# Seven of 31 convolution taps on VectorE, with two replica queues and the even layer's end reordered

## The reference

```python
def even_mixer(h, pos, w_in, conv_w, conv_b, ln_w, ln_b, ...):
    a_val, a_gate, q, k, v = _split(h @ w_in, [CONV_CH, CONV_CH, DIFF_QK, DIFF_QK, DIFF_V])
    u = a_val * jax.nn.sigmoid(a_gate)
    u = causal_depthwise_conv(u, conv_w) + conv_b.astype(u.dtype)   # 31 taps, 512 channels
    u = jax.nn.silu(layer_norm(u, ln_w, ln_b))                      # over the 512 channels
    q = partial_rotary(q.reshape(B_, S, 2 * DIFF_HEADS, DIFF_HEAD_DIM), pos)
    k = partial_rotary(k.reshape(B_, S, 2 * DIFF_HEADS, DIFF_HEAD_DIM), pos)
    ...
    o = diff_attention(q, k, v, lam)                 # 4 heads, (softmax 1 - lam * softmax 2) v
    o = rms_norm(o, subln_w) * (1.0 - lambda_init)
    return jnp.concatenate([u, o.reshape(B_, S, DIFF_V)], axis=-1)
...
        x = x + y @ w_out[l]
        h = rms_norm(x, ffn_norm_w[l])
        x = x + (jax.nn.silu(h @ w_gate[l]) * (h @ w_up[l])) @ w_down[l]
```

## Time and profile before

| | before |
|---|---|
| runs, us | 1342.91, 1343.10, 1343.13 |
| median, us | 1343.1 |
| profiled execution, us | 1342.96 |
| its span, first to last instruction, us | 1340.9 |
| PE busy, us | 1319.5 (98%) |
| DVE busy, us | 630.8 (47%) |
| ACT busy, us | 501.0 (37%) |
| mean granted TensorE clock | 0.989 |

### The profile page before, as it was taken

One profiled execution on the slowest core, in us unless ns is written; L12 is line 12 of the kernel. 1 busy time (PEld: TensorE's weight loads), 2 busy tenths in 40 slices (PEclk: granted clock), 3 DMA queues, 4 the chain that ended last, 5 costly groups with the idle time before them and its releaser, 6 DMA issues.

```text
span 1340.9 us, 17222 instructions
## 1 busy us (share of the span) xinstructions
PE 1319.5 (98%) x6507; PEld 1065.5 (79%) x6507; DVE 630.8 (47%) x898; ACT 501.0 (37%) x735; POOL 13.9 (1%) x22
## 2 busy tenths in 40 slices
PE   9999989999999999999999999999999999999997
PEld 6775637888888878888887988888888888878886
DVE  6664623744444442226757337433644444442224
ACT  6344423533333332115464344444433333332111
POOL 0000000000000000000001010000000000000000
PEclk9999988999999999999999999999999999999998
DMA  6222220322222223222321101001322222223221
GB/s 249 85 90 81 68 78 0 126 94 94 94 94 94 94 94 110 94 95 78 102 72 63 48 33 48 32 16 48 125 93 95 94 94 94 94 94 110 94 78 63
DMA packets 34079, 114.08 MB, mean 85 GB/s; under 512 B 4466, under 2 KB 4722, under 8 KB 34034
## 3 DMA queue, kind: packets, MB, share of 16 engines
q1 hardware_dynamic: 34034, 113.44, 25.1%
HBM read 106.90 MB, written 2.10 MB: 81 GB/s over the span
## 4 chain that ended last, share of the span: by engine, by line
PE 93%; ACT 2%; DVE 2%; DMA 1%; SPq 1%; issue 1%; DVEq 0%; ACTq 0%
PE PS L1325 91%; DMA raw<-w_stream 1%; PE PS L1401 1%; SPq L463 1%; PE PS L1740 1%; ACT wring L542 1%; DVE wring L930 1%; DVE hbuf L1173 0%; DVE outT L1319 0%; ACT HH L546 0%; PE PS L1621 0%; DMA reps<-ub 0%; ACT squares L554 0%; ACT G L758 0%; DVE ubuf L901 0%
## 5 line engine op out<-in xcount | busy, mean ns | idle before, releaser
L1325 PE MATMUL PS<-HH,wring 128*128 128x512 f32 x3096 | 730.2, 394 | 0.0
L1325 PEld LDWEIGHTS PS<-HH,wring 128*128 128x128 f32 x3096 | 576.6, 188 | 121.7 <-issue 4.2
L1325 PE MATMUL PS<-AA,wring 128*128 (+1 forms) x1320 | 305.3, 392 | 1.9 <-DVE ubuf L901 1.6
L1325 PEld LDWEIGHTS PS<-AA,wring 128*128 128x128 f32 x1320 | 248.4, 189 | 55.6 <-DVE ubuf L901 2.4
L901 DVE TENSOR_TENSOR ubuf<-PS,rstd 128x512 f32<-128x512 f32 x44 | 30.4, 691 | 198.2 <-PE PS L1325 198.2
L923 DVE TENSOR_TENSOR wring<-raw,wring 128x1024 fp32r<-128x1024 f32 x36 | 44.1, 1226 | 149.6 <-ACT wring L593 149.6
L910 DVE TENSOR_TENSOR wring<-raw,wring 128x1024 fp32r<-128x1024 f32 x88 | 107.5, 1221 | 0.9 <-ACT wring L585 0.4
L930 DVE TENSOR_TENSOR wring<-raw,wring 128x1024 fp32r<-128x1024 f32 x70 | 85.2, 1220 | 42.7 <-ACT wring L542 42.7
L542 ACT ACTIVATE wring<-raw 128x1024 fp32r<-128x1024 f32 x70 | 73.5, 1055 | 76.8 <-PE PS L1325 54.6
L580 ACT ACTIVATE AA<-ubuf 128x512 f32 x44 | 27.9, 633 | 198.2 <-DVE ubuf L908 198.2
L593 ACT ACTIVATE wring<-raw 128x1024 fp32r<-128x1024 f32 x36 | 38.2, 1061 | 155.6 <-PE PS L1325 151.2
(11 more groups left out here) (247 smaller groups left out, 1004.8 us busy)
## 6 DMA issues: line engine op xcount, KB each, us to landing
raw<-w_stream SPq DMA_DIRECT2D x194, 512.0 KB, 3.2
reps<-ub SPq DMA_DIRECT2D x64, 67.5 KB, 2.0
out_t<-outT SPq DMA_DIRECT2D x8, 256.0 KB, 2.2
xT<-x_t SPq DMA_DIRECT2D x3, 512.0 KB, 8.1
first_raw<-w_stream SPq DMA_DIRECT2D x2, 512.0 KB, 9.5
rope<-rope_const SPq DMA_DIRECT2D x1, 576.0 KB, 6.9
consts<-shape_const SPq DMA_DIRECT2D x1, 576.0 KB, 7.7
xT<-x_t SPq DMA_DIRECT2D x2, 256.0 KB, 3.9
```

The source lines that it names most:

```text
L1325: return nc.tensor.matmul(out, lhsT, rhs, start=start, stop=stop)
```

## The change

PE's share of the convolution falls from 31 taps (8 steps) to 24 (6 steps, three parts of two). The other seven taps are multiply-adds of 128 x 512 on DVE, one for each tap and channel block: the first with the bias by TENSOR_SCALAR, six by SCALAR_TENSOR_TENSOR, accumulating in `cacc`, each waiting for the one before. `TAP_SLOTS` says in which slot each stands: one in each slot from 3 to 11, more from 12 on (2, 2, 3, 2, 5, 4 in slots 12 to 17). DVE instead of ACT takes the products out of PSUM and adds them to `cacc`.

DVE sums the four channel blocks (`ln_add`, three adds) so that the layer norm's sum needs one product in place of four, and sums the four squares (`ln_sq_add`) so that the variance needs four small products in place of 16. Of the replicas of c2 and c3, SP issues eight transfers and ACT the other eight. A replica row is 532 floats in place of 540. The end of the layer is written in another order: the layer norm's sum and its centring come ahead of the last head's statistics, the variance ahead of the third output tile's products, and `ln_bc` ahead of the fourth's.

```diff
-GROUPS, SHIFTS, TAP_STEPS = 4, 4, 8
+GROUPS, SHIFTS, TAP_STEPS = 4, 4, 6
+FIRST_DIRECT = SHIFTS * TAP_STEPS
+DIRECT = TAPS - FIRST_DIRECT
+V_DIRECT = V_CONVW + 4 * GROUPS * TAP_STEPS
+TAP_SLOTS = ((3, 4, 5, 6, 7, 8, 8), (9, 10, 11, 12, 13, 14, 14), (12, 13, 14, 15, 15, 16, 16), (16, 16, 16, 17, 17, 17, 17))
...
+        taps = [("tap", (c, k)) for c in range(4) for k in range(DIRECT) if TAP_SLOTS[c][k] == n]
+        for part in range(3):
+            after[part] += taps[part * len(taps) // 3:(part + 1) * len(taps) // 3]
         for part in range(4):
             if kind == "c":
-                order.append(("conv", (slot[1], part)))
+                if part < TAP_STEPS // 2:
+                    order.append(("conv", (slot[1], part)))
...
+        if kind == "c" and slot[1]:
+            order.append(("ln_add", slot[1]))
+        if slot == ("g", 3, 1):
+            order.append(("replicate", 2))
+        if slot == ("c", 1):
+            order.append(("replicate", 3))
...
-                for g in range(GROUPS):
+                for g in range(GROUPS if c < 2 else GROUPS // 2):
                     sp.dma_start(dst[32 * sh:32 * sh + 32, g], ub[c % 2][32 * g:32 * g + 32, sh:sh + REP]).then_inc(sem(f"replicated{c}"), 16)
...
-            elif kind == "conv_evac":
-                act.wait_ge(sem("conv_mm"), a + 1)
-                nc.scalar.activation(cacc[:, a], PS[:, conv_bank(a)], ACT.Identity, bias=vcol(V_CONVB + a)).then_inc(sem("conv_done"), 1)
+            elif kind == "replicate":
+                act.wait_ge(sem("gated"), a + 1)
+                act.wait_ge(tile_used, T_OUT0)
+                for sh in range(SHIFTS):
+                    for g in range(GROUPS // 2, GROUPS):
+                        nc.scalar.dma_start(replicas[a][32 * sh:32 * sh + 32, g], ub[a % 2][32 * g:32 * g + 32, sh:sh + REP]).then_inc(sem(f"replicated{a}"), 16)
...
+            elif kind == "tap":
+                c, k = a
+                src = ub[c % 2][:, FIRST_DIRECT + k:FIRST_DIRECT + k + S]
+                weight = vcol(V_DIRECT + DIRECT * c + k)
+                if k == 0:
+                    dve.wait_ge(sem("gated"), c + 1)
+                    V.tensor_scalar(cacc[:, c], src, weight, vcol(V_CONVB + c), ALU.mult, ALU.add).then_inc(sem(f"direct{c}"), 1)
+                else:
+                    dve.wait_ge(sem(f"direct{c}"), k)
+                    V.scalar_tensor_tensor(cacc[:, c], src, weight, cacc[:, c], ALU.mult, ALU.add).then_inc(sem(f"direct{c}"), 1)
+            elif kind == "conv_evac":
+                dve.wait_ge(sem("conv_mm"), a + 1)
+                dve.wait_ge(sem(f"direct{a}"), DIRECT)
+                V.tensor_tensor(cacc[:, a], cacc[:, a], PS[:, conv_bank(a)], ALU.add).then_inc(sem("conv_done"), 1)
+            elif kind == "ln_add":
...
+                V.tensor_tensor(ln_total[:], cacc[:, 0] if a == 1 else ln_total[:], cacc[:, a], ALU.add).then_inc(sem("ln_added"), 1)
+            elif kind == "ln_sq_add":
...
+                V.tensor_tensor(lnsq[:, 0], lnsq[:, 0], lnsq[:, a], ALU.add).then_inc(sem("ln_sq_added"), 1)
...
             elif kind == "ln_sum":
-                pe.wait_ge(sem("conv_done"), 4)
+                pe.wait_ge(sem("ln_added"), 3)
                 pe.wait_ge(sem("y_scaled"), 2)
-                for c in range(4):
-                    last = mm(PS[:, LN_MEAN], ones, cacc[:, c], c == 0, c == 3)
-                last.then_inc(sem("ln_mean_mm"), 1)
+                mm(PS[:, LN_MEAN], ones, ln_total[:]).then_inc(sem("ln_mean_mm"), 1)
             elif kind == "ln_var_sum":
-                pe.wait_ge(sem("ln_sq"), 4)
+                pe.wait_ge(sem("ln_sq_added"), 3)
                 pe.wait_ge(sem("y_scaled"), 3)
                 for b in range(NB):
-                    for c in range(4):
-                        last = mm(PS[:, LN_VAR, b:b + 1], lnsq[:, c, blk(b)], ones[:, 0:1], c == 0, c == 3)
+                    last = token_sum(PS[:, LN_VAR, b:b + 1], lnsq[:, 0, blk(b)])
```

More of the change, by code:

```diff
@@ L144, in even_order @@
                 order.append(("val_gate", (n, part)))
-            order += after[part]
+            if part < 3 or n < 17:
+                order += after[part]
         order.append({"c": ("conv_evac", slot[1]), "q": ("qk_evac", slot[1]), "g": ("gate_evac", n)}[kind])
-    order += [("sub_lo", 2), ("sub_sum", 1), ("ln_sum", 0), ("sub_ms", 1), ("sub_root", 1), ("sub_rec", 1), ("out_heads", (0, 0, 3)),
-              ("sub_bc", 3)]
-    order += [("ln_centre", c) for c in range(4)]
-    order += [("sub_mul", 3), ("sub_hi", 3), ("sub_lo", 3), ("out_heads", (1, 0, 3)), ("out_heads", (2, 0, 3)), ("ln_var_sum", 0), ("out_heads", (3, 0, 3)), ("ln_var", 0), ("ln_root", 0),
-              ("ln_rec", 0), ("ln_bc", 0), ("out_heads", (0, 3, 4)), ("out_heads", (1, 3, 4)), ("out_heads", (2, 3, 4)), ("out_heads", (3, 3, 4))]
+        if kind == "c" and slot[1]:
[4 more added lines that the diff above has]
+            order.append(("replicate", 3))
+    order += after[3]
+    order += [("sub_lo", 2), ("ln_sum", 0)] + [("ln_centre", c) for c in range(4)]
+    order += [("out_heads", (0, 0, 2)), ("sub_sum", 1), ("out_heads", (0, 2, 3)), ("sub_ms", 1), ("sub_root", 1), ("sub_rec", 1),
+              ("ln_sq_add", 1), ("ln_sq_add", 2), ("out_heads", (1, 0, 3)), ("ln_sq_add", 3), ("sub_bc", 3), ("sub_mul", 3), ("sub_hi", 3),
+              ("sub_lo", 3), ("ln_var_sum", 0), ("out_heads", (2, 0, 3)), ("ln_var", 0), ("ln_root", 0), ("ln_rec", 0), ("ln_bc", 0),
+              ("out_heads", (3, 0, 3))]
+    order += [("out_heads", (n, 3, 4)) for n in range(4)]
     for c in range(4):
@@ L291, in build @@
     ub1, q = at("ub1", [PAD + S + 2], f32, q)
+    ln_total, _ = at("ln_total", [S], f32, q)
     reps, q = at("reps", [GROUPS, REP], f32, q)
@@ L1067, in _ @@
                 diff_combine(a)
+            elif kind == "tap":
[13 more added lines that the diff above has]
+            elif kind == "ln_add":
+                dve.wait_ge(sem("conv_done"), a + 1)
+                if a == 1:
+                    dve.wait_ge(sem("conv_mm"), 2)
+                else:
+                    dve.wait_ge(sem("ln_added"), a - 1)
+                V.tensor_tensor(ln_total[:], cacc[:, 0] if a == 1 else ln_total[:], cacc[:, a], ALU.add).then_inc(sem("ln_added"), 1)
+            elif kind == "ln_sq_add":
+                dve.wait_ge(sem("ln_sq"), a + 1)
+                if a > 1:
+                    dve.wait_ge(sem("ln_sq_added"), a - 1)
+                V.tensor_tensor(lnsq[:, 0], lnsq[:, 0], lnsq[:, a], ALU.add).then_inc(sem("ln_sq_added"), 1)
             elif kind == "ln_centre":
@@ L1476, in _ @@
                                   r == 0, r == TAP_STEPS - 1)
-                if part == 3:
+                if part == TAP_STEPS // 2 - 1:
                     last.then_inc(sem("conv_mm"), 1)
```

10 lines of the change are left out of this document (6 added, 4 removed).

## The result

| | before | after |
|---|---|---|
| runs, us | 1341.71 to 1343.13 (4) | 1328.06, 1328.11, 1330.62, 1331.17 |
| median, us | 1343.0 | 1329.4 |
| profiled execution, us | 1342.96 | 1331.17 |
| its span, us | 1340.9 | 1329.4 |

The ratio is 0.9907, with a 95% interval of 0.9895 to 0.9919. The forecast was 1329.2 us. The profiled execution is the slowest of its four, so its rows show a gain of 11.8 us where the medians show 13.7.

What follows compares the result with a forecast made beforehand. PE, busy 98% of the span, was taken to bound the kernel. Convolution 5.6, replicas 1.2 and end of the layer 8.9, less 1.85 of rotary stalls, gave 13.8 us off 1342.96: 1329.2 us, range 1325 to 1334.

Steps and rivals of the forecast that it cites:

- term for the clock behind the variance: End of the layer: the slow clock over the nine passes behind the variance goes, 1.9 us saved.
- c1 and the replicas: c1's saved part ends in the wait for c2's replicas, which land at 170.4 instead of 171.6: 1.2 us gained.
- Convolution, 5.6: PE drops one part of two tap steps in each of c0, c2 and c3: 3 x 1.86 = 5.6 us saved.
- ACT's eight stand behind the sigmoid: c2's replicas: ACT's transfers start after the last gate's sigmoid at 163.6, the last issued at 168.0, landing at 170.0 at best.
- Rotary products, 1.85: Taps on DVE delay evacuations that rotary products await: 0.77 us in slot 11, 0.92 in 12, 0.15 in 3; 1.85 lost.
- End of the layer, 8.9: Layer norm's end: saves 2.4 us on the sum, 1.2 on the squares' wait, 3.4 on the variance, 1.9 of slow clock.
- DVE's three adds of squares lie beside 12 passes and a spread: Before the variance: PE has other work during DVE's adds, so the wait for squares goes, 1.2 us saved.
- The DMA engines are the limit: Rival: both queues share what one fills, c2's replicas land at 171.6; +1.2 us, 1330.4, chance 0.10.
- The clock stays slow behind the variance: Rival: something in the new order rests PE behind the variance; +1.9 us, 1331.1, chance 0.06.
- the clock is better: Rival: c3's first part, or the stretch behind c2's wait, runs at full clock; 1.7 us less, 1327.5, chance 0.10.
- DVE falls behind: Rival: stalls at the rotary products are twice the forecast and c3's sum comes 2 us late; +3.8, 1333, chance 0.12.
- dear issues: Rival: transfers issued by ACT cost over 1.05 us each and delay PE; at worst 1344 to 1346 us, chance 0.05.

Runs made afterwards that it cites:

- load later: The changed kernel with SP waiting until c2's replicas have landed before issuing tile 24's load and its half of c3: 1323.81 us, ratio 0.9889.
- one queue: The changed kernel with all 16 replica transfers of c2 and of c3 issued by SP, none by ACT: 1327.54 us, ratio 0.9907.
- Taps moved: The changed kernel with taps of c1 and c2 in earlier or later slots, none in slots 11 and 12: 1326.22 us, ratio 0.9904.
- combined: The changed kernel with tile 24 and SP's c3 half held back, no taps in slots 11 and 12, one-column sums spread, variance later: 1322.79 us, again 1321.59.

## Why the prediction was right, step by step

- **The sum was right, in part by parts that offset each other.** Without its term for the clock behind the variance (1.9) it says 11.9 us; work and waits gave 11.8. With the clock's losses taken out of the table of milestones, the stretch to c1 brought 0.5 us for a forecast 0, c1 and the replicas 1.5 for 1.2, c2 and c3 4.1 for 3.7, and the end of the layer 5.9 for 7.0. That the medians show 1.9 us more, just the clock's term, is luck: the profiled pair differs by 0.2 us in clock.
- **Convolution, 5.6: right in work, short in this profile.** c2 and c3 bring 1.0 and 1.1 us in the table of milestones, not 1.86 each. c2's first two parts took 5.34 for 5.04, by the clock; the 24 one-column passes took 3.38 for 2.77, and the slow clock behind them reached past c3's transposes to 188.2. That is 2.0 us more slow clock than in before; without it the two parts bring 4.1.
- **c1 and the replicas, 1.2: right in size, wrong in mechanism.** The step that failed is "ACT's eight stand behind the sigmoid" and are paced by issuing. ACT issues ahead of its arithmetic, so the last one left 2.4 us earlier, at 165.64 for 168.0, and the landing took 4.58 us for 2.0, among other transfers. That the two errors cancel is luck. The gain in this step was 1.5. My doubt, tile 24 and SP's half of c3 beside ACT's half, was the cause of the late landing, and load later priced it at 2.4 us.
  The rule of the Trainium skill (DMA: Bandwidth & Descriptors, Rules for kernel authors) says that more issuing engines bring no bandwidth and save only issue time. Its second half agrees with one queue's 1.5 us. Its first half fits the longer landing at a share of 0.87, but was not tested by itself.
- **ACT's issues: right.** The median was 0.613 us, 0.86 the longest, and c3 did not wait in after.
- **Rotary products, 1.85: 1.41.** 0.81 and 0.60 us for the forecast 0.77 and 0.92; slot 3 cost nothing. Taps moved gave 1.5 to 2.0 back.
- **DVE's taps: right.** Chained ones took 0.747 us for 0.77 (mean of 24). The first took 0.54 for 0.49: the bound from the earlier trace rows was near, not exact. (Slot 8 holds two taps, not one as the section on the change says; c0's are complete there.)
- **End of the layer, 8.9: 9.3, of which 3.4 are the clock's.** Before lost 3.4 us to slow clock in that stretch and after none, where the forecast counted on 1.9. Work and waits brought 5.9 for the forecast 7.0. The step "DVE's three adds of squares lie beside 12 passes and a spread" failed: PE waited 1.01 us, since I checked PE's cover and not the chain from the value product over ACT and DVE. Of the 2.4 for the sum 1.0 to 1.2 are real, of the 3.4 for the variance under 2. The slow clock behind the variance went in one profile of the changed kernel and came in the other, so the term of 1.9 has no ground in the order.
- **The rivals.** "The DMA engines are the limit" was half right: they set the landing, yet two queues still brought time. "The clock stays slow behind the variance" and, for c3's first part, "the clock is better" turned out to vary between executions of one order; the slow stretch behind c2's wait stayed with the wait, as the prediction said. "DVE falls behind" did not come: the stalls were under mine. Nor did dear issues.

## What to carry over

When work is taken off the engine that sets the time, walk the chain of the other engines up to each result it will need, and not only the work it has left to cover it. Before adding a second queue for an urgent transfer, see which transfers that nobody awaits yet go beside it, and hold those back. Where the clock's losses fall differently in each run, compare waits in the trace and the length without those losses; the time alone hides an edit of 1 to 2 us. Count as lost only slow clock in which the engine had work. And look whether one of the slow stretches keeps to a wait: then shortening the wait may pay twice.

## What the runs showed of the hardware

- ACT's sequencer issued transfers while ACT's arithmetic instructions ahead of them were still running: at 161.04 us, beside a copy that ran until 161.79 and ahead of a table load and a sigmoid. The last four came when the sigmoid had ended, and what held them until then is open. An issue took 0.51 to 0.86 us.
- A transfer of 66.5 KB whose median landing is 2.2 us took 4.58 with the DMA engines at a share of 0.87 (after), and 2.1 when the load behind it was held back (load later).
- TensorE's slow clock took 2.1 to 10.6 us up to PE's last instruction, in pieces of about 1.7, most of them at places that change between executions of one kernel. Most was lost in before, least in the second profile of combined (2.1) and with 31 taps on PE (2.3), which have no slow stretch from 165 to 230 us.
- Over the first 1.2 us behind the replica wait the granted clock was 0.50 to 0.65 in all eight profiles with a wait of 3.04 to 4.89 us, and 1.00 in all five with one of 0.83 to 1.23 us.
